# A transformer-and-recurrence step on one core: token-half norms, three tiles opened at once, a fourth weight slot

## The chip, the cores and the metric

The kernel runs on one core of a Trainium2 chip. A core has five engines that work side by side, each through its own instructions in order: TensorE (PE) multiplies matrices into PSUM, VectorE (DVE) and ScalarE (ACT) do elementwise work and read PSUM out, GpSimd (POOL) does elementwise work on SBUF, and SyncE (SP) issues most transfers. They meet only at semaphores. The metric is the device time of one execution in microseconds, the median of three runs.

## The reference

The reference is one inference step of a two-layer trunk. All tokens (16 meta, 512 prompt, 64 sample: 592 in all) go through one matrix product after another, and after each of the four sublayers stands a layer norm over the 1024 features, whose result is what the next product reads:

```
for layer in range(DEPTH):
    if layer % 2 == 0: m, ... = _mixer_ret_hgrn(x, ...)      # 32 tiles in, 8 tiles out
    else:              m, ... = _mixer_rglru(x, ...)         # 16 tiles in, 8 tiles out
    x = _layernorm(DEEPNORM_ALPHA * x + m, ...)              # norms 0 and 2
    f, nb = _conv_ffn(x, ...)                                # gelu(conv(x @ up_u)) * (x @ up_v), then @ down
    x = _layernorm(DEEPNORM_ALPHA * x + f, ...)              # norms 1 and 3

def _layernorm(x, g, b):
    mu = xf.mean(-1, keepdims=True)
    var = jnp.mean(jnp.square(xf - mu), -1, keepdims=True)
    return (xf - mu) * lax.rsqrt(var + LN_EPS) * g + b
```

## The kernel before

Features lie on the 128 partitions and tokens along the free axis, so x is eight rows of 592 tokens. Every weight matrix is cut into units: one unit gives 128 output features from eight (in a down-projection six or eight) blocks of 128 input features. Weights and activations are split into a high and a low part (`whi`, `wlo`, `xhi`, `xlo`, for the down-projections `hhi`, `hlo`), and `products` multiplies high by high, low by high and high by low: three matmuls of 296 columns for each block and each half of the tokens, so 48 matmuls for a unit of eight blocks. All units of the kernel stand in one sequence `u`.

The weights of a unit go through a chain: SP loads them into one of two `raw` buffers, ACT copies them to `whi` (`weights_hi`), DVE subtracts to get `wlo` (`weights_lo`), in one of three slots, and only then may PE begin the unit. Where `weights_hi(u + 2)` and `weights_lo(u + 2)` stand in the lists of ACT and DVE is written out by hand, unit by unit. The sums of a unit go to one of two accumulators in PSUM (two banks each, one for each token half); the semaphore `full` says that PE is done with it, `free` that ACT or DVE has read it.

A down-projection ends in a norm. Each of its last eight units adds to a row of `Y` (`add_tile`), DVE keeps the running sum Z0 and the sum of squares Z1, and ACT makes the squares. The last unit (`last_tile`) is done by token halves: first all blocks for tokens 0 to 295, then those for 296 to 591, with the matmuls that turn Z0 and Z1 into mean and mean square (`layer_norm_moments`, L675) for the first half after the sixth block of the second half. From there on the first half of the tokens goes through variance, Ln and Exp (for the reciprocal root), then row by row through DVE (subtract the mean L1308, scale L1311), ACT (bias L877, then `xhi` L879) and POOL (`xlo` L478). `first_tiles` opens the next two units together: at each block that arrives it does the products of both units for that half of the tokens, and in the second half the second unit runs three blocks behind.

After the norm ACT's list goes on with `weights_hi` of the third unit, then reads out the first unit (in a feed-forward network L912 to L918, in the recurrent mixer L984 to L989), then `weights_hi` of the fourth. DVE's list goes on with `weights_lo` of the third, then the convolution of the first unit, then `weights_lo` of the fourth. The feed-forward network has 22 u/v pairs of units in groups of 8, 8 and 6, each group followed by eight down units of as many blocks. Its `u` units are convolved, its `v` units multiplied by the gelu.

## Time and profile before

| | us |
|---|---|
| median of 3 runs | 1509.72 (1508.63 to 1510.45) |
| the profiled execution | 1509.73 |
| its span, first to last instruction | 1507.9 |
| PE busy in the span | 1439.3 |
| DVE busy | 849.3 |
| ACT busy | 622.7 |
| POOL busy | 61.0 |

The profiled execution lies 1.8 us over its span and agrees with the median. The busy share is an average over stages. To see what sets the time, look at the stretches around each norm and ask for each what PE waited for there; the stretches between the norms can be read in one row each.

### The profile page before, as it was taken

To read this page: it belongs to the slowest core of one execution; us is meant where nothing else is said; L and a number is where in the kernel's file an instruction comes from. 1 tells how busy PE (TensorE), PEld (TensorE's weight loads), DVE (VectorE), ACT (ScalarE), POOL (GpSimd) and SP (SyncE) were. 2 spreads that over 40 slices of the span, in tenths; PEclk is the share of its full clock that TensorE was granted. 3 is DMA by queue.
4 is the path that set the end of the run, shared out by engine and by line. 5 is a ranking of instruction groups with operands and counts; after the bars stand their busy time and mean duration, and the time that the engine had idled before them with its cause. 6 is when DMAs were issued, how large, how long until landed. Compare 5 with 4: busy or idle time off the path is not lost.

```text
span 1507.9 us, 24289 instructions
## 1 busy us (share of the span) xinstructions
PE 1439.3 (95%) x10240; PEld 1402.7 (93%) x10240; DVE 849.3 (56%) x1290; ACT 622.7 (41%) x1018; POOL 61.0 (4%) x80
## 2 busy tenths in 40 slices
PE   6999999999899999999999899998999999999993
PEld 6989898989899999999999799997999999999993
DVE  4566564755665554553355877868645344524556
ACT  4443544443464313341243676736543133313433
POOL 0010000000110000000000300002000000000000
PEclk9999999999999999999999999999999999999997
DMA  7132222323222222222222122121222222222222
GB/s 261 54 90 83 72 87 72 94 89 113 84 76 79 85 85 82 73 84 85 80 72 74 57 85 70 57 84 43 85 85 84 85 71 84 84 85 71 78 63 80
DMA packets 37085, 125.22 MB, mean 83 GB/s; under 512 B 4208, under 2 KB 6384, under 8 KB 36720
## 3 DMA queue, kind: packets, MB, share of 16 engines
q1 hardware_dynamic: 33264, 112.32, 23.3%
q0 software_dynamic: 2560, 8.91, 2.1%
q10 hardware_dynamic: 1152, 2.43, 0.5%
q8 instruction: 81, 1.33, 0.3%
q14 instruction: 28, 0.23, 0.0%
HBM read 115.95 MB, written 7.70 MB: 82 GB/s over the span
## 4 chain that ended last, share of the span: by engine, by line
PE 85%; DVE 6%; ACT 5%; DMA 1%; issue 1%; SPq 0%; POOL 0%; ACTq 0%; DVEq 0%
PE PS L486 26%; PE PS L487 26%; PE PS L488 26%; PE PS L713 1%; DMA C<-consts 1%; ACT Y L877 1%; PE PS L628 1%; ACT xhi L879 1%; PE PS L587 1%; DVE Y L1311 1%; DVE S L1209 1%; DVE wlo L1063 1%; PE PS L608 1%; DVE Y L1308 1%; PE PS L643 1%
## 5 line engine op out<-in xcount | busy, mean ns | idle before, releaser
L486 PE MATMUL PS<-xhi,whi 128*128 128x296 f32 x2176 | 668.8, 307 | 21.6 <-POOL xlo L478 6.9
L487 PE MATMUL PS<-xlo,whi 128*128 128x296 f32 x2176 | 656.1, 302 | 0.0
L488 PE MATMUL PS<-xhi,wlo 128*128 128x296 f32 x2176 | 653.3, 300 | 0.0
L486 PEld LDWEIGHTS PS<-xhi,whi 128*128 128x128 f32 x2176 | 413.9, 190 | 33.5 <-POOL xlo L478 14.6
L487 PEld LDWEIGHTS PS<-xlo,whi 128*128 128x128 f32 x2176 | 414.1, 190 | 1.2 <-issue 0.2
L488 PEld LDWEIGHTS PS<-xhi,wlo 128*128 128x128 f32 x2176 | 413.3, 190 | 0.0
L1063 DVE TENSOR_TENSOR wlo<-raw,whi 128x1024 fp32r<-128x1024 f32 (+1 forms) x198 | 238.2, 1204 | 111.8 <-ACT whi L744 108.4
L486 PE MATMUL PS<-hhi,whi 128*128 128x296 f32 x960 | 288.8, 301 | 4.2 <-ACT S L1015 3.0
L487 PE MATMUL PS<-hlo,whi 128*128 128x296 f32 x960 | 288.6, 301 | 0.0
L488 PE MATMUL PS<-hhi,wlo 128*128 128x296 f32 x960 | 287.5, 299 | 0.0
L744 ACT ACTIVATE whi<-raw 128x1024 fp32r<-128x1024 f32 (+1 forms) x198 | 206.5, 1043 | 175.2 <-PE PS L488 166.0
L486 PEld LDWEIGHTS PS<-hhi,whi 128*128 128x128 f32 x960 | 181.8, 189 | 5.4 <-issue 5.1
L487 PEld LDWEIGHTS PS<-hlo,whi 128*128 128x128 f32 x960 | 181.5, 189 | 0.4
L488 PEld LDWEIGHTS PS<-hhi,wlo 128*128 128x128 f32 x960 | 181.5, 189 | 0.0
L1345 DVE TENSOR_SCALAR S<-S,W 128x608 f32<-128x608 f32 x44 | 26.2, 596 | 149.9 <-ACT S L915 149.9
L925 ACT ACTIVATE hhi<-S 128x592 fp32r<-128x592 f32 x44 | 30.8, 700 | 145.4 <-DVE S L1359 145.4
L1348 DVE SCALAR_TENSOR_TENSOR S<-S,W 128x608 f32<-128x608 f32 x88 | 75.0, 852 | 3.1
L912 ACT ACTIVATE S<-W 128x16 f32<-128x16 f32 x44 | 9.6, 219 | 147.9 <-PE PS L488 147.9
L1273 DVE TENSOR_TENSOR Y<-PS,Y 128x592 f32<-128x592 f32 x30 | 23.3, 775 | 81.7 <-PE PS L488 81.7
L478 POOL TENSOR_TENSOR xlo<-Y,xhi 128x296 fp32r<-128x296 f32 x48 | 39.5, 823 | 666.0 <-ACT xhi L879 664.4
L853 ACT ACTIVATE S<-Y 128x592 f32<-128x592 f32 x28 | 19.6, 701 | 104.6 <-DVE Y L1271 58.1
L1271 DVE SCALAR_TENSOR_TENSOR Y<-Y,PS 128x592 f32<-128x592 f32 x30 | 23.1, 771 | 68.6 <-PE PS L488 68.4
(208 smaller groups left out, 1121.6 us busy)
## 6 DMA issues: line engine op xcount, KB each, us to landing
raw<-weights SPq DMA_DIRECT2D x182, 512.0 KB, 3.5
raw<-weights SPq DMA_DIRECT2D x16, 384.0 KB, 3.0
Y<-xP SPq DMA_DIRECT2D x8, 296.0 KB, 8.7
Y<-xT ACTq DMA_DIRECT2D x8, 296.0 KB, 4.1
yT<-Y SPq DMA_DIRECT2D x16, 148.0 KB, 1.8
C<-consts SPq DMA_DIRECT2D x1, 2146.5 KB, 15.3
S<-s_hgrn POOLq DMA_DIRECT2D x4, 512.0 KB, 4.6
S<-s_ret POOLq DMA_DIRECT2D x4, 512.0 KB, 4.8
```

The costliest lines, as they stand in the source:

```text
L478: pool.tensor_tensor(xlo[:, m, span(half)], Y[:, m, span(half)], xhi[:, m, span(half)].bitcast(F32), ALU.subtract).then_inc(x_lo, 1)
L486: pe.matmul(dst, wh, h, start=first, stop=False)
L487: pe.matmul(dst, wh, lo, start=False, stop=False)
L488: return pe.matmul(dst, wl, h, start=False, stop=last)
L744: act.activation(whi[:, u % SLOTS, 0:n], raw[:, u % RAWS, 0:n], ACT.Copy).then_inc(w_hi, 1)
L853: done(act.activation(s(T0 + m % 2), Y[:, m, :], ACT.Square), sq_ok)
L925: done(act.activation(hhi[:, j - first, :], s(4 + j % 2), ACT.Copy), h_hi)
L1063: tt(wlo[:, u % SLOTS, 0:n], raw[:, u % RAWS, 0:n], whi[:, u % SLOTS, 0:n].bitcast(F32), ALU.subtract).then_inc(w_lo, 1)
L1271: done(stt(y, y, ALPHA, a, ALU.mult, ALU.add), free[u % 2], u // 2 + 1)
L1273: done(tt(y, a, y, ALU.add), free[u % 2], u // 2 + 1)
L1345: done(ts(y, r[:, 0:n], par("ffn_conv_w", (layer * FW) * FT + j), par("ffn_conv_b", layer * FT + j), ALU.mult, ALU.add))
L1348: done(stt(y, r[:, q:q + n], par("ffn_conv_w", (layer * FW + q) * FT + j), y, ALU.mult, ALU.add), conv if q == FW - 1 else None)
```

## The change

1. The last two units of a down-projection are done by token halves (`last_tiles`): first half of both, then second half of both. The sums Z0 and Z1 for the first half are turned to moments after the fifth block of the second half of the last unit but one. For the second half of the tokens the last two rows are not added to Z0 and Z1: `moments_of_second_half` gives PE three rows to add up for each of mean and mean square, six matmuls in place of two. In norms 0 to 2 they stand in `first_tiles`, after its fourth step; in norm 3 right behind the last unit.
2. `first_tiles` opens three units in three accumulators. In the first half of the tokens they run 0, 3 and 6 blocks behind each other, in the second half side by side. The feed-forward networks go on with three accumulators, the mixers with two.
3. There are four weight slots in place of three, and the weights of the next three units are prepared earlier: `ahead` gives which at each of the last units. In `ffn` and in the mixer's loop `weights_hi(u + 2)` and `weights_lo(u + 2)` are left out for the first unit, so the fourth unit's come at the second.
4. DVE subtracts the mean for one or two rows at a time (`NORM_ROWS`), from a copy of the mean in SBUF that ACT makes; the reciprocal root stays in SBUF. ACT writes `xhi` for the rows of a group in one instruction. In norm 3 DVE only subtracts and multiplies, two rows at a time, and ACT applies gain and bias.
5. Groups of 6, 8 and 8 in place of 8, 8 and 6; in the recurrent mixer four gates and two decays come one unit later. `Sc` lies in rows of `S`.

```diff
-GROUPS = [8, 8, 6]
+GROUPS = [6, 8, 8]
...
-LAG = 3
+LAGS = [0, 3, 6]
+NORM_ROWS = [[(0, 1), (1, 2), (3, 2), (5, 2), (7, 1)], [(0, 2), (2, 2), (4, 2), (6, 2)]]
...
-GATES_AFTER = {2: 0, 3: 1, 5: 2, 6: 3, 9: 4, 10: 5, 12: 6, 13: 7}
+GATES_AFTER = {3: 0, 4: 1, 6: 2, 7: 3, 9: 4, 10: 5, 12: 6, 13: 7}
...
+def ahead(u, m):
+
+    return [u + 2] if m < KT - 3 else {KT - 3: [u + 2, u + 3], KT - 2: [u + 3], KT - 1: []}[m]
...
-        RAWS, SLOTS = 2, 3
+        RAWS, SLOTS = 2, 4
...
+            def last_tiles(u, ln):
+
+                n = unit_tiles(u)
                 for half in range(2):
+                    for i in range(2):
+                        for k in range(n):
+                            half_product(u + i, half, k, hhi, hlo, first_half)
+                            if half and i == 0 and k == n // 2:
+                                moments_of_first_half(ln)
+                if ln == 3:
+                    moments_of_second_half(ln)
...
+            def first_tiles(u, ln):
+
+                for half in range(2):
+                    lags = LAGS if half == 0 else [0, 0, 0]
+                    for step in range(KT + max(lags)):
+                        if step < KT:
+                            pe.wait_ge(x_lo, KT * (1 + 2 * ln + half) + step + 1)
+                        for i, lag in enumerate(lags):
+                            if 0 <= step - lag < KT:
+                                half_product(u + i, half, step - lag, xhi, xlo)
+                        if half == 0 and step == 3:
+                            moments_of_second_half(ln)
...
+            def moments_of_second_half(ln):
+
+                rows = [(s(Z0), Y[:, KT - 2, :], Y[:, KT - 1, :]), (s(Z1), s(T0), s(T1))]
+                pe.wait_ge(y_half, 4 * ln + 4)
+                pe.wait_ge(sq_ok, (KT + 2) * ln + KT + 2)
+                pe.wait_ge(mu_ok, 2 * ln + 1)
+                pe.wait_ge(var, 2 * ln + 1)
+                for i in range(2):
+                    for j, row in enumerate(rows[i]):
+                        mm = pe.matmul(PS[:, 6 + i, 0:HT], const("mean_d"), row[:, HT:T], start=j == 0, stop=j == 2)
+                mm.then_inc(ln_ps, 1)
...
+                square(KT - 2, 0)
+                square(KT - 1, 0)
+                mean(0)
                 root(0)
...
+                shifted(0, 0)
+                square(KT - 2, 1)
+                shifted(0, 1)
+                square(KT - 1, 1)
+                weights_hi(u + 3)
+                shifted(0, 2)
+                mean(1)
+                shifted(0, 3)
+                root(1)
+                shifted(0, 4)
+                for i in range(len(NORM_ROWS[1])):
+                    shifted(1, i)
...
-                    if i < N_FFN - 1:
+                    if kind == "d" and g == len(GROUPS) - 1:
+                        for v in ahead(u, j):
+                            weights_hi(v)
+                    elif i:
                         weights_hi(u + 2)
...
             for i, (kind, m) in enumerate(MIXER):
-                weights_hi(U_RNN + i + 2)
+                if i:
+                    weights_hi(U_RNN + i + 2)
...
                     if kind == "u":
-                        weights_lo(u + 2)
+                        if i:
+                            weights_lo(u + 2)
```

Three places show what moves. The first is ACT's list behind norm 0, where the first feed-forward unit is read out (the last rows of the norm are the pairs that end in `xhi`; `whi<-raw` is a unit's high weights). Before, the weights of the third unit and, behind the read-out, those of the fourth:

```order
L877 ACTIVATE Y<-Y,W 128x296
L879 ACTIVATE xhi<-Y 128x296
L744 ACTIVATE whi<-raw 128x1024
L912 ACTIVATE S<-W 128x8x2
L913 ACTIVATE S<-PS 128x8x8
L914 ACTIVATE S<-PS 128x296
L915 ACTIVATE S<-PS 128x232
L916 ACTIVATE KV<-PS 128x2
L918 ACTIVATE KV<-PS 128x16
L744 ACTIVATE whi<-raw 128x1024
L923 ACT_TABLE_LOAD
```

And in the changed kernel:

```order
L938 ACTIVATE Y<-Y,W 128x296 x2
L940 ACTIVATE xhi<-Y 128x2x296
L981 ACTIVATE S<-W 128x8x2
L982 ACTIVATE S<-PS 128x8x8
L983 ACTIVATE S<-PS 128x296
L984 ACTIVATE S<-PS 128x232
L985 ACTIVATE KV<-PS 128x2
L987 ACTIVATE KV<-PS 128x16
L799 ACTIVATE whi<-raw 128x1024
L992 ACT_TABLE_LOAD
```

The third unit's `whi` is gone from ahead of the read-out (it has moved into the norm), and the fourth unit's still stands behind it.

The second is DVE's list at the same place; `wlo<-raw,whi` is a unit's low weights, the rows on `S<-S,W` are the convolution of the first unit. Before:

```order
L1308 TENSOR_TENSOR Y<-Y,PS 128x296
L1311 SCALAR_TENSOR_TENSOR Y<-Y,W,PS 128x296
L1335 MEMSET S 128x2 x2
L1063 TENSOR_TENSOR wlo<-raw,whi 128x1024
L1345 TENSOR_SCALAR S<-S,W 128x608
```

And in the changed kernel:

```order
L1394 TENSOR_TENSOR Y<-Y,S 128x2x296
L1407 SCALAR_TENSOR_TENSOR Y<-Y,W,S 128x296 x2
L1435 MEMSET S 128x2 x2
L1446 TENSOR_SCALAR S<-S,W 128x608
L1449 SCALAR_TENSOR_TENSOR S<-S,W 128x608 x2
L1134 TENSOR_TENSOR wlo<-raw,whi 128x1024
```

The convolution now comes first, and the low weights behind it are the fourth unit's.

The third is ACT's list inside the norm. `S<-PS` is what reads the moments of the second half of the tokens. Before, it reads them behind the second row:

```order
L877 ACTIVATE Y<-Y,W 128x296
L879 ACTIVATE xhi<-Y 128x296
L865 ACTIVATE S<-PS 128x296
L877 ACTIVATE Y<-Y,W 128x296
L879 ACTIVATE xhi<-Y 128x296
```

And in the changed kernel, from the group of rows 1 and 2 on:

```order
L938 ACTIVATE Y<-Y,W 128x296 x2
L940 ACTIVATE xhi<-Y 128x2x296
L916 ACTIVATE S<-Y 128x296
L799 ACTIVATE whi<-raw 128x1024
L938 ACTIVATE Y<-Y,W 128x296 x2
L940 ACTIVATE xhi<-Y 128x2x296
L920 ACTIVATE S<-PS 128x296
L921 ACTIVATE S<-PS 128x296
L938 ACTIVATE Y<-Y,W 128x296 x2
```

The third unit's weights stand between rows 2 and 3, and the moments of the second half (L920 squares the mean, L921 copies it) ahead of rows 5 and 6. On PE those moments stand behind the products that wait for row 3:

```order
L523 MATMUL PS<-xhi,whi 128x296 [waits x_lo_ready]
L524 MATMUL PS<-xlo,whi 128x296
L525 MATMUL PS<-xhi,wlo 128x296
L523 MATMUL PS<-xhi,whi 128x296 [waits acc0_free,weights_lo]
L524 MATMUL PS<-xlo,whi 128x296
L525 MATMUL PS<-xhi,wlo 128x296
L734 MATMUL PS<-S,C 128x296 [waits ln_mean_in_sbuf,ln_var_ready,y_squared,last_tile_half_added]
L734 MATMUL PS<-Y,C 128x296 x2
L734 MATMUL PS<-S,C 128x296 x3
L523 MATMUL PS<-xhi,whi 128x296 [waits x_lo_ready]
```

Before, they stood at the end of the last unit, ahead of everything that `first_tiles` does.

## Rows read from the trace of the kernel before

**Rows 1.** The page's head: engine busy us (share) and instructions.

```profile
PE 1439.3 (95%) x10240; PEld 1402.7 (93%) x10240; DVE 849.3 (56%) x1290; ACT 622.7 (41%) x1018; POOL 61.0 (4%) x80
```

**Rows 2.** Table by stretches: start:end, length, busy us (instructions) by engine, PE clock, DMA.

```profile
386.90:432.31 45.41, 39.65 (x250) 35.73 (x249) 34.47 (x61) 30.93 (x57) 13.16 (x16) 0.96 0.17 52
834.96:877.76 42.80, 36.61 (x227) 32.61 (x226) 35.56 (x62) 29.64 (x60) 13.18 (x16) 0.96 0.19 57
1023.48:1068.46 44.98, 39.69 (x250) 36.06 (x249) 35.93 (x63) 30.82 (x57) 13.19 (x16) 0.96 0.15 50
1471.11:1507.90 36.79, 13.56 (x82) 11.68 (x80) 24.91 (x47) 15.01 (x27) 0.00 (x0) 0.70 0.23 82
432.31:834.96 402.65, 402.65 (x2955) 402.65 (x2953) 195.94 (x276) 134.56 (x240) 0.00 (x0) 1.00 0.26 81
```

**Rows 3.** Timeline of PE through norm 0: start, us, engine, line, [idle before <-releaser].

```profile
399.16 1.16 PE L675 MATMUL PS<-S,C 128*128 128x296 f32 x4
...
403.99 2.34 PE L675 MATMUL PS<-S,C 128*128 128x296 f32 x4 [2.85 <-DVE S L1254]
405.70 0.88 PE L486 MATMUL PS<-xhi,whi 128*128 128x296 f32 x1
...
425.68 0.37 PE L486 MATMUL PS<-xhi,whi 128*128 128x296 f32 x1 [0.30 <-ACT KV L918]
```

**Rows 4.** Timeline of ACT, DVE and POOL from the moments to the first x row.

```profile
400.35 0.42 ACT L865 ACTIVATE S<-PS 128x296 f32<-128x296 f32 x1 [1.34 <-PE PS L675]
401.36 0.54 ACT L870 ACTIVATE S<-S,C 128x296 f32<-128x296 f32 x1 [0.59 <-DVE S L1304]
403.52 0.54 ACT L877 ACTIVATE Y<-Y,W 128x296 f32<-128x296 f32 x1 [0.69 <-DVE Y L1311]
404.10 0.45 ACT L879 ACTIVATE xhi<-Y 128x296 fp32r<-128x296 f32 x1
...
402.91 0.52 DVE L1311 SCALAR_TENSOR_TENSOR Y<-Y,W,PS 128x296 f32<-128x296 f32 x1
...
404.70 0.81 POOL L478 TENSOR_TENSOR xlo<-Y,xhi 128x296 fp32r<-128x296 f32 x1 [51.07 <-ACT xhi L879]
```

**Rows 5.** Instructions over both halves of a row, DVE and ACT, before norm 0.

```profile
394.53 0.78 DVE L1278 TENSOR_TENSOR S<-S,Y 128x592 f32<-128x592 f32 x1
...
394.53 0.70 ACT L853 ACTIVATE S<-Y 128x592 f32<-128x592 f32 x1 [4.75 <-DVE Y L1271]
```

**Rows 6.** Timeline behind norm 0: read-out of the first unit, weights, convolution.

```profile
423.79 0.22 ACT L912 ACTIVATE S<-W 128x16 f32<-128x16 f32 x1 [0.73 <-PE PS L488]
...
425.57 1.06 ACT L744 ACTIVATE whi<-raw 128x1024 fp32r<-128x1024 f32 x1
...
425.15 0.60 DVE L1345 TENSOR_SCALAR S<-S,W 128x608 f32<-128x608 f32 x1 [0.76 <-ACT S L915]
425.79 1.74 DVE L1348 SCALAR_TENSOR_TENSOR S<-S,W 128x608 f32<-128x608 f32 x2
427.56 1.23 DVE L1063 TENSOR_TENSOR wlo<-raw,whi 128x1024 fp32r<-128x1024 f32 x1
```

**Rows 7.** Timeline of DVE behind norm 1: convolution of the mixer's first unit.

```profile
870.58 0.60 DVE L1437 TENSOR_SCALAR S<-S,W 128x616 f32<-128x616 f32 x1 [0.78 <-ACT S L987]
...
874.13 1.23 DVE L1063 TENSOR_TENSOR wlo<-raw,whi 128x1024 fp32r<-128x1024 f32 x1
```

**Rows 8.** Table by stretches around waits of PE (columns as in rows 2).

```profile
403.70:407.10 3.40, 3.12 (x8) 2.49 (x9) 2.42 (x6) 2.52 (x6) 1.62 (x2) 0.50 0.00 0
1485.70:1507.90 22.20, 2.34 (x4) 1.17 (x4) 15.97 (x33) 10.04 (x19) 0.00 (x0) 0.50 0.38 134
330.00:334.40 4.40, 1.66 (x13) 1.42 (x13) 1.27 (x3) 3.00 (x6) 0.00 (x0) 1.00 0.86 270
407.10:425.70 18.60, 15.69 (x94) 12.88 (x93) 14.95 (x31) 16.46 (x38) 11.53 (x14) 1.00 0.04 5
```

**Rows 9.** Timeline of ACT at the end: its last row.

```profile
1503.75 0.54 ACT L877 ACTIVATE Y<-Y,W 128x296 f32<-128x296 f32 x1 [0.51 <-DVE Y L1311]
```

More of the change, by code:

```diff
@@ new lines, in shifted @@
+                def shifted(half, i):
+                    first, n = NORM_ROWS[half][i]
+                    for m in range(first, first + n):
+                        act.wait_ge(ln_c, (2 * ln + half) * KT + m + 1)
+                        y, b = Y[:, m, span(half)], par(f"ln_{which}_b", layer * KT + m)
+                        if ln == 3:
+                            g = par(f"ln_{which}_g", layer * KT + m)
+                            done(act.activation(y, y, ACT.Identity, scale=g, bias=b), ln_x)
+                        else:
+                            done(act.activation(y, y, ACT.Identity, bias=b), ln_x)
```

305 lines of the change are left out of this document (163 added, 142 removed).

## The prediction, made before the changed kernel was run

> **What bounds the kernel now.** I read the page's head first: PE is busy 95% of the span, nothing else over 56% [rows 1]. So the time is PE's work plus the places where PE has none, and the change can gain only in those. The table by stretches says where they are [rows 2]. The stretch between two norms (432.31 to 834.96, and one of the same length in the second layer) is busy to the last 0.01 us: 2955 matmuls in 402.65 us, 0.1363 us each. The four stretches around the norms are not. For each I start where the last unit but one of the down-projection starts (call this point S) and stop where the fourth unit after the norm starts. By the number of matmuls such a stretch should take five units, 32.71 us at 48 x 0.1363 (29.44 in norm 1, whose two last units have six blocks), and it took 45.41, 42.80 and 44.98: 12.70, 13.36 and 12.27 us over. In the last stretch there are 9.81 us of units, and with 36.79 us it is 26.98 over. Those 65.3 us are what the change works on.
>
> Then I looked at what PE waits for in one of them. In norm 0 PE waits 2.85 us for the sum of squares of the second half, and works on x from 405.70 on at the pace at which rows arrive; at the third unit it waits 0.30 us more [rows 3]. The row's path is ACT, DVE, ACT, POOL [rows 4].
>
> **Parts that cost or gain nothing.** The third accumulator and the fourth slot inside the feed-forward networks remove no wait, since the stretch is full [rows 2]. Groups of 6, 8, 8 hold the same blocks as 8, 8, 6; what moves is 3.27 us of units into stretch 2 and into the last, which the count "over the units" takes care of. The first down units now take 6 x 6 x 0.1363 = 4.91 us; DVE's three or four operations there, 0.8 to 1.2 us each [rows 5, 6], fit. The heads' order is as before.
>
> **Norm 0, step by step.** All times are from S.
>
> Both first halves are full at 48 x 0.1363 = 6.54. DVE and ACT then need add, sum, square, add again; by their durations at one half (about 0.47 each) the sums are there at 8.2. PE comes to the first moments 15 matmuls after 6.54, at 8.59, and doesn't wait. This is the part that works: 33 of the 96 matmuls are still to come and cover the chain; PE's last one ends at 14.3 (96 x 0.1363 and 1.2 for the moments). In the old order the path from moments to the first matmul on x took 405.70 - 399.16 = 6.54 us [rows 3]; the new one loses one DVE subtract ahead of it and takes 6.2. So x row 0 is used at 14.8: PE waits 0.5 us where it waited 2.85 and then for 1.7 us of moments.
>
> But then PE lives on arrivals. For each row ACT spends 0.54 on the bias and 0.45 on `xhi` (0.70 for two rows at once) [rows 4, 5], POOL 0.81 [rows 4]. Into the same ACT list the change puts two squares (0.45 each) and the third unit's high weights (1.06 [rows 6]) ahead of row 3. Walked one after the other: rows 1, 2 and 3 reach PE at 17.1, 17.9 and 20.3. PE has 0.41 us of products for each of rows 0 to 2 (only the first unit is open), so it waits 1.7, 0.3 and 1.9 us.
>
> Now the second moments. They are six matmuls where there were two. Two took 399.16 to 400.35, the first products behind them starting 0.77 us after [rows 3, 4], so I take 0.25 for each half of one and 12 x 0.25 = 3.0 us. They stand on PE behind row 3, from 21.2 to 24.2. ACT reads them ahead of the bias of rows 5 and 6, so all of ACT's list waits for PE: mean squared and mean (0.42 each), two biases, one `xhi`, POOL; row 5 is there at 28.3. PE has used up row 4 by 25.1 and waits 3.2 us. In the old order the moments needed nothing from `first_tiles`.
>
> From 28.3 on PE has enough to do: 17 products of three matmuls left in the first half, 24 in the second, 41 x 0.409 and about a tenth of a us for each of eleven waits: 46.2.
>
> There the second halves of all three units end together. The fourth unit needs its weights. ACT's list has the read-out of the first unit, then `weights_hi`; DVE's has its convolution, then `weights_lo` (both as the order shows). The first unit is full 0.82 us before 46.2; read-out to L915 takes 423.79 to 425.12, convolution 0.60 and 1.74, weights 1.23 [rows 6]: 46.2 - 0.8 + 0.2 + 1.4 + 2.4 + 1.2 + 0.2 = 50.8. PE waits 4.6 us. Before, this wait was 0.30, as the third unit's weights stood ahead of the read-out and the third unit's 6.54 us covered the rest.
>
> So the fourth unit starts at 50.8, 18.1 over its units, against 12.7: **5.4 us lost**. Walked by the same durations the old order comes out 0.3 us short of its trace.
>
> **Norm 1** has the same walk, but the mixer's convolution is longer (870.58 to 874.13, 3.5 us [rows 7]): the last wait is 5.7, 19.2 over against 13.4: **5.8 lost**. In **norm 2** DVE restores three rows of x (0.78 each [rows 5]) and makes two `wlo` while the unit ahead of S runs, and is about 1.3 us late: 18.7 over against 12.3: **6.4 lost**. Together 17.6.
>
> **The clock.** After a wait of 2.85 us PE ran at half its clock (1.2 GHz) for 3.4 us [rows 3, 8]; each of the three stretches shows this as a mean of 0.96 [rows 2]. After a wait of 2.74 at 330 to 334 it did not, nor in the stretch full of waits under 0.9 (407.10 to 425.70) [rows 8]. In the new order each norm has two waits longer than the 2.85 that half clock followed (3.2 and 4.6) and PE is dense behind both, so each stretch of half clock costs up to half of 3.4, 1.7 us. I take 1.25 for each of two, less the 0.3 of the old order: 2.2 a norm, **6.6 in all**; the bounds are 0 and 1.7 x 3 x 3 = 15, with a third one over the loose stretch from 14 to 21, where PE is busy a third of the time.
>
> [...]
>
> **Norm 3.** The chain of the first half is the same up to 12.0. Behind it stands no PE work but 3.0 us of moments, which wait for the last squares until 16.0 (DVE's add and ACT's square behind 14.3). DVE's work on two rows is 0.78 + 0.78 where it was four of about 0.5; ACT (0.54 a row) keeps up. The second moments end at 19.0, variance and root 2.2 us later; then four groups of 1.6 on DVE, and ACT's last two: 29.2. The old list ended at 1504.29 [rows 9], 33.2 from S, with 3.27 less of units. From the end of ACT to the end of the span stay 3.6 us. So 16.1 over against 23.4: **7.3 gained**, less 0 to 3 for moments at half clock (they took 2.34 for four there [rows 3]); I take 1.0, **6.3**.
>
> **The sum** against the profiled time: 1509.7 + 17.6 + 6.6 - 6.3 = 1527.6, and the median of the runs is the same 1509.7. I say 1527.5.
>
> **Rivals.**
> (a) Faster: the head start does what it is for, so that waits end with row 3. This needs the moments read without holding ACT's list and the fourth unit's weights ready. Then PE is dense from 20.3: 45 products, 3.0 of moments and 1.3 of small waits end at 43.0, and the fourth unit starts at 43.5, 10.8 over: 1.9, 2.6 and 1.5 gained, with the end 12 us, 1497.5. For it: PE has the work. Against it: both orders are written out, and engines don't overtake in their lists. It decides if the two waits of 3.2 and 4.6 us shrink by more than 6 us together in each norm, a third of the 17.9 that the sum is over. 4%.
> (b) Only the fourth unit's weights come in time: 14 us less wait and half of the clock's cost, 1510 to 1513, about as before. Against: the same list. 6%.
> (c) More is lost than I count: half clock three times a norm, 9 us more, 1536. For it the loose stretch; against it rows 8's 407.10 to 425.70, busy 84% though. 17%.
> (d) The mixer falls behind: DVE's second convolution stands behind the fourth unit's weights while PE goes on at once, and by the order ACT loads its tables 16 times there for 14. A list that gets behind by one convolution, 3.5 us [rows 7], can make PE wait once for a gate or for a free accumulator: 0 to 3.5 us more. I count nothing, as the fourth unit's own 6.5 us and a gate's products cover it. Otherwise 1531. 13%.
> The forecast itself, 1521 to 1533: 60%.
>
> **How the numbers follow.** The range is 1517 to 1537: below, no clock cost (1521) less an error of 1 us a norm; above, most of (c). What this kernel's measurement can tell from no change is about 0.2%, 3 us. Faster by more: (a), 4%, and a miss in the same direction, 2%: 6%. Within: (b), 5%. Slower: 89%.
>
> **What would show it.** The trace of the changed kernel should have, in each of norms 0 to 2, a wait of about 0.5 us at the first product on x; one near 3.2 us at the products for row 5, with ACT idle until the six-matmul moments end; and 4 to 6 us before the fourth unit, with `wlo` as releaser. Stretches of half clock behind those two. From S to the fourth unit it should take about 53, 54 and 53.5 us. The dense stretches should stay at 0.1363 a matmul. From the last matmul of the last unit to the end: about 18.5 us, where it was some 25. If the wait before the fourth unit is missing, I have misread the lists; if the wait for row 5 is missing, the moments or what stands behind them are cheaper than I think.

## The result, and the profile after

The changed kernel is slower: a median of 1542.39 us in four runs against 1509.43 for the kernel before beside it, a ratio of 1.0213 (95%: 1.0194 to 1.0231). Its four runs lie in two pairs, 1538.27 and 1538.78, 1546.01 and 1546.43. The profiled one is 1538.78, and everything below explains that one. Run again as e0 it gave 1537.78 (1536.35 to 1538.77), without the upper pair. So the forecast of 1527.5 is 10 to 15 us short, and the time lies outside the range that ended at 1537.

The head of the profile after, engine busy us (share) and instructions, answers to [rows 1]:

```profile
PE 1453.8 (95%) x10272; PEld 1418.3 (92%) x10272; DVE 854.8 (56%) x1251; ACT 628.7 (41%) x1011; POOL 66.1 (4%) x80
```

PE is busy 14.5 us longer. The 32 more records are the added matmuls of the second moments, four in each norm with two records each, 8.0 us at the 0.25 of the forecast. The other 6.5 us are work that was there before and now takes longer.

The table by stretches of the kernel after, with columns as in [rows 2]: the stretch from S to the fourth unit in norms 0, 1 and 2, the end, and then the stretch between norms 0 and 1, which in the kernel before was full and at full clock:

```profile
388.03:441.35 53.32, 41.84 (x258) 38.45 (x256) 34.57 (x48) 28.33 (x50) 14.89 (x16) 0.88 0.11 34
842.93:897.01 54.08, 40.65 (x259) 37.61 (x257) 35.66 (x50) 29.56 (x58) 14.90 (x16) 0.93 0.10 32
1045.41:1099.50 54.09, 42.09 (x259) 38.96 (x257) 35.56 (x50) 28.31 (x50) 14.90 (x16) 0.89 0.11 33
1501.36:1537.00 35.64, 19.14 (x114) 16.95 (x112) 20.49 (x32) 17.65 (x30) 0.00 (x0) 0.78 0.24 84
441.35:842.93 401.58, 401.58 (x2928) 401.58 (x2929) 199.19 (x281) 137.28 (x243) 0.00 (x0) 0.99 0.27 83
```

With them the account of the span (1507.9 to 1537.0, 29.1 us more) closes:

| | before | after | difference |
|---|---|---|---|
| up to S of norm 0 | 386.90 | 388.03 | +1.1 |
| S to fourth unit, norms 0 to 2 | 45.41, 46.07, 44.98 | 53.32, 54.08, 54.09 | +25.0 |
| between the norms (three stretches) | 399.38, 145.72, 399.38 | 401.58, 148.40, 401.86 | +7.4 |
| S of norm 3 to the end | 40.06 | 35.64 | -4.4 |

Where units moved with the groups, the 3.27 us that they take are put where they are now: norm 1 before is 42.80 + 3.27, the end 36.79 + 3.27, and the long stretches 402.65 - 3.27.

The third line is new. Most of it is the clock. The stretch behind the fourth unit splits like this (same view, after):

```profile
439.10:445.92 6.82, 4.57 (x18) 4.57 (x19) 5.47 (x9) 5.23 (x10) 0.00 (x0) 0.50 0.26 77
448.00:842.90 394.90, 394.90 (x2897) 394.90 (x2896) 193.93 (x273) 132.89 (x234) 0.00 (x0) 1.00 0.27 82
```

From 439.1 to 445.9 PE has half its clock, 1.2 GHz, and for the last 4.57 us of it PE is dense, which costs 2.3. Then 394.90 us go by at 0.1363 a matmul as before. In the trace of the kernel before, each of norms 0 to 2 has one stretch of half clock of 3.4 us. Now norm 0 has 10.2 us (from 405.0) and 6.8 us (from 439.2), norm 1 has 6.8 and 3.4, norm 2 has 6.8, 3.4 and 6.8.

The waits, on the other hand, are the forecast's. Timeline of PE through norm 0 after (as [rows 3]): the first products on x rows 0, 1 and 3, the six matmuls of the second moments, the first product on row 5, and the first of the fourth unit:

```profile
402.67 0.40 PE L523 MATMUL PS<-xhi,whi 128*128 128x296 f32 x1 [0.42 <-POOL xlo L515]
405.25 0.61 PE L523 MATMUL PS<-xhi,whi 128*128 128x296 f32 x1 [1.91 <-POOL xlo L515]
409.18 0.61 PE L523 MATMUL PS<-xhi,whi 128*128 128x296 f32 x1 [1.83 <-POOL xlo L515]
410.83 1.19 PE L734 MATMUL PS<-S,C 128*128 128x296 f32 x2
...
413.78 2.40 PE L734 MATMUL PS<-S,C 128*128 128x296 f32 x6
419.92 0.41 PE L523 MATMUL PS<-xhi,whi 128*128 128x296 f32 x1 [2.93 <-POOL xlo L515]
441.35 0.61 PE L523 MATMUL PS<-xhi,whi 128*128 128x296 f32 x1 [4.40 <-DVE wlo L1134]
```

Two things are to be seen. The waits are 0.42, 1.91, 1.83, 2.93 and 4.40. And the matmul at 405.25 takes 0.61 where a full-clock one takes 0.40: from row 1 on PE is at half clock, and the six moments, which start at 410.83, are done only 5.4 us later, at 416.2, when ACT can read them.

ACT's side of the wait for row 5, and ACT's and DVE's sides of the wait for the fourth unit, in the timeline of norm 0 after:

```profile
416.22 0.42 ACT L920 ACTIVATE S<-PS 128x296 f32<-128x296 f32 x1 [8.33 <-PE PS L734]
...
437.20 0.37 ACT L984 ACTIVATE S<-PS 128x232 f32<-128x232 f32 x1
...
438.02 1.06 ACT L799 ACTIVATE whi<-raw 128x1024 fp32r<-128x1024 f32 x1
...
437.67 0.60 DVE L1446 TENSOR_SCALAR S<-S,W 128x608 f32<-128x608 f32 x1 [6.84 <-ACT S L984]
438.30 1.74 DVE L1449 SCALAR_TENSOR_TENSOR S<-S,W 128x608 f32<-128x608 f32 x2
440.07 1.22 DVE L1134 TENSOR_TENSOR wlo<-raw,whi 128x1024 fp32r<-128x1024 f32 x1
```

ACT is idle for 8.33 us although rows 5 to 7 of the first half wait for it: its next instruction reads the mean of the second half, which PE has not yet made. Later DVE is idle for 6.84 us and then does the convolution ahead of the `wlo` that PE is waiting for. This is the whole list effect. The second moments are also where the slow clock hurts a second time, since ACT waits for them.

The last piece stands in the groups of instructions: line, engine, operation, count | busy us, mean ns of one. After, the POOL low part and the DVE scale by the reciprocal root:

```profile
L515 POOL TENSOR_TENSOR xlo<-Y,xhi 128x296 fp32r<-128x296 f32 x48 | 44.7, 949 | 690.8 <-ACT xhi L940 690.8
L1407 DVE SCALAR_TENSOR_TENSOR Y<-Y,W,S 128x296 f32<-128x296 f32 x48 | 40.3, 840 | 4.7 <-ACT S L927 3.2
```

and the same two groups of the kernel before:

```profile
L478 POOL TENSOR_TENSOR xlo<-Y,xhi 128x296 fp32r<-128x296 f32 x48 | 39.5, 823 | 666.0 <-ACT xhi L879 664.4
L1311 DVE SCALAR_TENSOR_TENSOR Y<-Y,W,PS 128x296 f32<-128x296 f32 x64 | 33.5, 523 | 2.3
```

The same operations on the same shapes have become dearer on both engines, 823 to 949 ns and 523 to 840. The one difference is that the root is now read from SBUF (`Y<-Y,W,S` for `Y<-Y,W,PS`).

### The profile page after: what moved, and what is told of

It is laid out like the page before. It is cut to its first block, busy times and chain, and to the rows that moved or that the text cites. A ratio compares the mean times of both kernels' runs of the same rounds, so it can differ in the third digit from the quotient of the medians.

```text
span 1537.0 us, 24403 instructions
## 1 busy us (share of the span) xinstructions
PE 1453.8 (95%) x10272; PEld 1418.3 (92%) x10272; DVE 854.8 (56%) x1251; ACT 628.7 (41%) x1011; POOL 66.1 (4%) x80
## 4 chain that ended last, share of the span: by engine, by line
PE 82%; DVE 9%; ACT 5%; issue 1%; DMA 1%; SPq 0%; POOL 0%; ACTq 0%; DVEq 0%
PE PS L523 25%; PE PS L524 25%; PE PS L525 25%; DVE wlo L1134 1%; PE PS L734 1%; DMA C<-consts 1%; PE PS L675 1%; DVE Y L1407 1%; PE PS L634 1%; DVE S L1280 1%; PE PS L655 1%; PE PS L690 1%; DVE S L1540 1%; ACT whi L799 1%; DVE S L1577 1%
## 5 line engine op out<-in xcount | busy, mean ns | idle before, releaser
L523 PE MATMUL PS<-xhi,whi 128*128 128x296 f32 x2176 | 670.2, 308 | 50.9 <-POOL xlo L515 22.3
L1134 DVE TENSOR_TENSOR wlo<-raw,whi 128x1024 fp32r<-128x1024 f32 (+1 forms) x198 | 237.9, 1204 | 93.6 <-ACT whi L799 89.6
L515 POOL TENSOR_TENSOR xlo<-Y,xhi 128x296 fp32r<-128x296 f32 x48 | 44.7, 949 | 690.8 <-ACT xhi L940 690.8
L1457 DVE TENSOR_TENSOR S<-PS,S 128x296 f32<-128x296 f32 x44 | 20.5, 466 | 68.2 <-PE PS L525 68.2
```

The lines of the kernel that those rows point to most:

```text
L515: pool.tensor_tensor(xlo[:, m, span(half)], Y[:, m, span(half)], xhi[:, m, span(half)].bitcast(F32), ALU.subtract).then_inc(x_lo, 1)
L523: pe.matmul(dst, wh, h, start=first, stop=False)
L1134: tt(wlo[:, u % SLOTS, 0:n], raw[:, u % RAWS, 0:n], whi[:, u % SLOTS, 0:n].bitcast(F32), ALU.subtract).then_inc(w_lo, 1)
L1457: done(tt(ht[:, 0:HT], a[:, 0, 0:HT], y[:, 0:HT], ALU.mult))
```

## The experiments

Eleven kernels were run. The questions were: how much does each of the two list waits cost, how much the clock, is anything else in the change good or bad, and can it be mended? Unless it is said otherwise, a diff is against the changed kernel. Each ratio is to the kernel before, run beside it.

### e0: the changed kernel again

> The changed kernel once more, in five rounds. Its four runs lay in two groups, 1538.3 and 1538.8, and 1546.0 and 1546.4, with mean clocks of 0.977 and 0.972. Theory (the clock): the two groups come again, about 8 us apart, since how much of the norms PE does at half clock depends on where its waits fall. Rival (the chip of those runs): one group only. From the second last unit to the fourth after the norm the profile should have 53.3, 54.1 and 54.1 us again if it falls in the lower group.

Measured: 1537.78 (1536.35 to 1538.77), ratio 1.0177 (1.0162 to 1.0192). The profiled execution of the first result belongs to this group. The two groups that were expected did not come again, so the expectation's rival (one group only) held. All differences below are taken to 1537.8.

### e1: the fourth unit's weights ahead of the read-out

```diff
@@ ACT, ffn
-                    elif i:
+                    elif i == 0:
+                        weights_hi(u + 3)
+                    elif i > 1:
                         weights_hi(u + 2)
@@ DVE, ffn
-                        if i:
-                            weights_lo(u + 2)
+                        weights_lo(u + (2 if i else 3))
...
-                        weights_lo(u + 2)
+                        if i > 1:
+                            weights_lo(u + 2)
```

and in the mixer's loops likewise.

> The changed kernel with the fourth unit's high and low weights ahead of the read-out and the convolution of the first unit, in the two networks and the mixer. Theory (the lists): the waits before the fourth unit (4.4, 5.6 and 4.4 us on wlo) shrink to 1.2 to 1.3 each, which are the read-out of the first unit, whose accumulator the fourth takes; 10.5 us less. With the shorter waits the half clock behind them, which cost about 2.4 us each outside the stretch, goes too: 7 us more, so 1521. Rival (the lists behind are late): ACT and DVE have the read-outs of three units to do, and the fifth or sixth unit waits instead, so that most comes back: 1532 or more.

Measured: 1524.25 (1523.61 to 1526.01), ratio 1.009 (1.0075 to 1.0105), so 13.5 us less. Waits of PE in e1, by what they wait for: us, count, mean; and the stretch of norm 0:

```profile
PE PS L523 <- POOL xlo L515: 21.9, 13, 2.9
...
PE PS L523 <- ACT KV L989: 2.2, 2, 1.1
```

```profile
387.69:437.71 50.02, 41.85 (x258) 38.45 (x257) 33.21 (x45) 26.13 (x48) 14.89 (x16) 0.90 0.15 48
```

In the kernel after the same view has this, with the wait for `wlo` second:

```profile
PE PS L523 <- POOL xlo L515: 22.3, 14, 2.9
...
PE PS L523 <- DVE wlo L1134: 14.4, 3, 5.6
```

Three waits of 4.40 to 5.6 us, 14.4 together, have turned into three of 1.1 for the read-out of an accumulator (`KV`), and the waits for rows are almost untouched (21.9 for 22.3). The stretches took 50.02, 49.59 and 50.51. The half clock behind the fourth unit is gone. The wait has two successors, though. Besides the 1.1 us for the accumulator, the two feed-forward networks now wait for the fifth unit's weights, since those come one convolution later:

```profile
PE PS L523 <- DVE wlo L1136: 3.3, 2, 1.7
```

So the three stretches are 11.4 us shorter and the long ones behind them keep 401.41 (399.38 before): the 2 us of half clock that went were taken by this wait. That is why it is 1524 and not the 1521 expected. The mechanism of the forecast's last wait is confirmed.

### e2: ACT reads the second moments two groups of rows later

```diff
@@ ACT
-                mean(1)
                 shifted(0, 3)
-                root(1)
                 shifted(0, 4)
+                mean(1)
+                root(1)
```

with DVE's `variance(1)` behind its fifth group to match.

> The changed kernel with ACT reading the second moments (mean, then variance and root) behind rows 5, 6 and 7 in place of ahead of rows 5 and 6, and DVE's variance moved the same way. Theory (ACT's list waits for PE): the wait for row 5 (2.9 us in each of three norms) goes and nothing takes its place, since PE has 41 block products ahead: 8.8 us less, 1530, and up to 4 less if a stretch of half clock goes with it. Rival: the root of the second half comes later and PE waits for its first rows instead, 1 to 3 us each: 1535 to 1538.

Measured: 1527.07 (1522.35 to 1527.82), ratio 1.01 (1.0083 to 1.0117), 10.7 us less. Waits of PE in e2:

```profile
PE PS L523 <- DVE wlo L1134: 14.4, 3, 5.6
PE PS L523 <- POOL xlo L515: 13.7, 11, 2.3
```

The waits for rows fall from 22.3 to 13.7, by 8.6 us (three of 2.92 are 8.8), and those for `wlo` don't move. The stretches took 50.16, 50.81 and 49.62. The wait at row 5 was indeed ACT standing at the moments. The stretches give 10.9 us. The end gives 2.1 more, 33.53 for 35.64 (0.3 of it by the edit, which reaches norm 3 too, the rest by the clock; see e5), and the mixer behind norm 1 takes 2.6 back, with a stretch of half clock of 6.8 us from 998.3 where the kernel after has 3.4.

### e5: the waits kept, the clock held

The kernel after with matmuls of constants put into PE's waits, whose result nothing uses: four ahead of rows 1 and 3, eight ahead of row 5, twelve ahead of the fourth unit in each of norms 0 to 2.

```diff
+            def filler(n, out):
+                for _ in range(n):
+                    pe.matmul(out, const("mean_d"), const("cos", 0, 200), start=True, stop=True)
...
+                        if half == 0 and step == 1:
+                            pe.wait_ge(free[ACC[u + 2]], NTH[u + 2])
+                        if half == 0:
+                            filler({1: 4, 3: 4, 5: 8}.get(step, 0), acc[ACC[u + 2]][:, 0, 0:200])
...
+                filler(12, PS[:, 6, 0:200])
```

> The changed kernel with added matmuls on a constant, whose result nobody reads, put in where PE waits: 4 ahead of rows 1 and 3, 8 ahead of row 5, 12 ahead of the fourth unit, in norms 0 to 2 (84 fp32 matmuls of 200 columns, 0.33 us each). They do no work of the computation. Theory (the clock is the part that I had too small): PE stays at full clock in the norms, the second moments take 3 us in place of 6 and the fourth unit starts at 0.1363 us a matmul: 2.5 us inside each stretch and 2.4 behind it, 14 to 15 us less, 1524. Rival (the waits alone): the clock stays or the fillers themselves cost what they save: 1538 or more.

Measured: 1522.58 (1520.38 to 1523.05), ratio 1.0072 (1.0055 to 1.0089), **15.2 us less with added work**. The stretches of the three norms in e5 (the last number but two is the clock; a constant matmul has two records, so 28 of them are some 56 more):

```profile
387.24:437.62 50.38, 47.92 (x315) 45.02 (x313) 34.53 (x48) 28.23 (x50) 14.88 (x16) 1.00 0.11 36
837.13:888.67 51.54, 47.90 (x314) 45.02 (x313) 35.64 (x50) 29.46 (x58) 14.90 (x16) 1.00 0.11 35
1036.94:1087.83 50.89, 48.19 (x314) 45.05 (x312) 35.64 (x50) 28.24 (x50) 14.91 (x16) 1.00 0.11 36
```

The clock is 1.00 in all three, where it was 0.88, 0.93 and 0.89. DVE's, ACT's and POOL's columns are those of the kernel after: nothing was moved but PE's own time. The second moments in e5:

```profile
409.31 0.66 PE L743 MATMUL PS<-S,C 128*128 128x296 f32 x2
...
410.81 1.66 PE L743 MATMUL PS<-S,C 128*128 128x296 f32 x6
412.08 0.52 PE L523 MATMUL PS<-xhi,whi 128*128 128x296 f32 x1
```

ACT's read of them begins at 412.50, 3.2 us after their start, about as the prediction had it (3.0), against 5.4 in the kernel after. PE still stood or ran fillers for 4.55, 5.77 and 4.55 us ahead of the fourth unit, so the waits on the other engines are unchanged. Between the two profiled executions (1538.78 and 1523.05) the 15.7 us are: 8.6 in the three stretches (2.9, 2.5, 3.2), 4.4 in the two long stretches, which are back at 399.51 and 399.52, 1.8 in the end, 0.1 in the mixer and 0.8 ahead of S of norm 0, where there are no fillers and which stays unexplained. The end has no fillers either, but there it is the clock. Timeline of PE at the end of e5, the second moments of norm 3:

```profile
1503.54 0.74 PE L743 MATMUL PS<-S,C 128*128 128x296 f32 x2 [1.97 <-issue]
...
1505.11 1.66 PE L743 MATMUL PS<-S,C 128*128 128x296 f32 x6
```

3.2 us, where the kernel after needs 4.9 for them (its rows stand below). Whether these moments fall into a stretch of half clock seems not to depend on the work around them: in after, e1, e2, e4, e5 and e9 they start 16.2 us behind S, after the same work. The end took 35.6 us in after, e1 and e6, 33.9 in e5, 34.4 in e9 and 33.5 to 33.6 in e2, e3, e4 and e10, whose edit has ACT read the moments of norm 3 later too and accounts for 0.3. This is the disputed cost by itself: **half clock costs about 15 us here**, 13.0 of which the fillers themselves took out (8.6 and 4.4). The prediction had put 7.6 in its sum (6.6 and 1.0 for norm 3), with 15 and 3 as bounds.

### e3: e1 and e2 together

The edits of both, and no other.

> Both moves of order together: the fourth unit's weights ahead of the read-out, and ACT's and DVE's reading of the second moments behind rows 5 to 7. Alone they took 13.5 and 10.7 us off 1537.8. Theory (two separate waits): they add up, 1513 to 1514, still above the kernel before, because the loose stretch at rows 0 to 3 and the longer moments stay. Rival (each frees the other's cover): less than the sum, 1518 or more.

Measured: 1512.49 (1511.78 to 1518.05), ratio 1.0015 (1.0006 to 1.0024). From e0 that is 25.3 us less, where 13.5 and 10.7 add up to 24.2. The stretches took 46.40, 46.08 and 47.23. So the two waits account between them, with the clock that each of them brings, for nearly all that the change lost; but 2.0 of the 25.3 are the end, where most of it is where the clock happened to fall. The profiled execution is 2.3 us over that of the kernel before: 3.3 more in the three stretches, 4.1 in the long ones (401.41 each, the waits for the fifth unit), 1.5 in the mixer and ahead of the first norm, and 6.5 less at the end.

### e4: e3, and the units staggered in the second half too

```diff
@@ against e3
-                    lags = LAGS if half == 0 else [0, 0, 0]
+                    lags = LAGS
```

> As the one with both moves, and the second half of the tokens with units 3 and 6 blocks behind each other as the first half has. Theory: the first unit is full 2.5 us before the third's last block, so its read-out (1.2 us exposed in each norm) is covered, and rows of the second half have fewer products waiting on them: 3 to 4 us less than with both moves alone, about 1510, near the kernel before. Rival: with rows of the second half arriving every 1.4 us (POOL and DVE block each other) PE runs out of products and waits there: no gain or a loss, 1513 to 1516.

Measured: 1509.53 (1508.58 to 1511.18), ratio 0.9993 (0.9984 to 1.0002), the same as before. The first unit now ends earlier than the others, and its read-out is done when PE wants the accumulator: the wait before the fourth unit is 0. The long stretches are back at 399.38 and 399.39. For that small waits for rows come back in the second half (0.32, 0.78 and 0.51 us in norm 0), since PE again runs at their pace, and the three stretches take 48.16, 47.93 and 47.28, 6.9 us more than before and 3.7 more than in e3. What e4 gains on e3 comes from the long stretches (4.1) and the mixer (145.05 for 146.62). Against the kernel before, the end, 33.59 for 40.06, pays for the stretches.

### e6: only two units opened

```diff
-LAGS = [0, 3, 6]
+LAGS = [0, 3]
...
-                    lags = LAGS if half == 0 else [0, 0, 0]
+                    lags = LAGS if half == 0 else [0, 0]
```

The third unit is done like any other. All else is as in the changed kernel.

> The changed kernel with two units opened together in place of three (0 and 3 blocks behind in the first half, side by side in the second), all else as changed, the third unit behind them. Theory: the third unit's 6.5 us cover the fourth unit's weights, so the 14.4 us of waits before the fourth unit go; but in the first half PE has fewer products behind row 5, and the third unit's start waits for the read-out of nothing (a third accumulator is free): 10 to 13 us less than changed, 1525 to 1528. Rival (three opened is what the gain rests on): PE waits for rows in both halves as before, and the time stays above 1532.

Measured: 1526.89 (1526.19 to 1528.52), ratio 1.0102 (1.0087 to 1.0117). Waits of PE in e6 have no entry for `wlo` L1134, and for rows

```profile
PE PS L523 <- POOL xlo L515: 26.6, 23, 2.9
```

Without the third unit the waits for rows rise by 4 us (22.3 to 26.6) and the wait of 4.4 to 5.6 before the fourth unit goes, since the third unit's own 6.5 us cover it. Taken as it was written, opening three units cost 11 us: it gave PE 4 us of work while rows were missing, and took away the cover of the next step. The clock behind the fourth unit is part of the 11: the long stretches take 399.40 each here for 401.58 and 401.86.

### e7: the groups alone, in the kernel before

```diff
-GROUPS = [8, 8, 6]
+GROUPS = [6, 8, 8]
```

> The kernel before with groups of 6, 8, 8 alone. Theory: two units of 8 blocks ahead of norms 1 and 3 cover DVE's running sums, so the wait of 0.79 and 0.85 us at the first moments goes, and 12 more matmuls cover the chain of the first half: 1.6 to 2.5 us less, 1508.5 to 1509.5 beside 1511.0. Rival: nothing that the rounds can tell (within 0.5 us).

Measured: 1508.27 (1506.36 to 1509.65), ratio 0.998 (0.9972 to 0.9989), 2.4 us less. In its waits of PE

```profile
PE PS L675 <- DVE S L1254: 11.9, 4, 3.3
```

where the kernel before has six such waits of 13.6 us together.

Two blocks more in the last unit cover two of the waits for the last sums. The prediction had counted the groups at nothing in the changed kernel, where last units are done by halves and such waits are gone. That isn't contradicted; the part is a small gain only on its own.

### e8: the root in SBUF, in the kernel before

```diff
-                    done(act.activation(PS[:, 6 + half, 0:HT], v, ACT.Exp, scale=-0.5), ln_r)
+                    done(act.activation(v, v, ACT.Exp, scale=-0.5), ln_r)
...
-                    done(stt(y, y, par(f"ln_{which}_g", layer * KT + m), rstd_of[half], ALU.mult, ALU.mult), ln_c)
+                    done(stt(y, y, par(f"ln_{which}_g", layer * KT + m), s(T1)[:, span(half)], ALU.mult, ALU.mult), ln_c)
```

> The kernel before with the reciprocal root written to its row in SBUF in place of PSUM, so that DVE's scale reads two operands from SBUF. Theory (DVE and POOL hold each other up when both read SBUF): DVE's scale grows from 0.52 us to about 1.0 where POOL runs beside it and POOL's low part from 0.82 to 0.9 and more, rows arrive every 1.4 us in place of 1.05, and each of norms 0 to 2 gets 1 to 4 us longer: 1514 to 1520 beside 1510.7. Rival: the slower rows of the changed kernel come from its two-row groups, and here the durations and the time stay.

Measured: 1514.99 (1513.08 to 1516.64), ratio 1.0026 (1.0016 to 1.0037), 4.5 us more. The two groups of instructions in e8:

```profile
L478 POOL TENSOR_TENSOR xlo<-Y,xhi 128x296 fp32r<-128x296 f32 x48 | 46.3, 990 | 663.8 <-ACT xhi L879 663.8
L1311 DVE SCALAR_TENSOR_TENSOR Y<-Y,W,S 128x296 f32<-128x296 f32 x64 | 36.1, 564 | 2.3
```

One operand moved from PSUM to SBUF, the same count of instructions and the same values, and POOL's operation goes from 823 to 990 ns; PE's waits for `xlo` go from 6.9 to 9.9 us. I had expected DVE's operation to bear it, at about 1 us. It goes only from 523 to 564: in this order of work POOL bears it. The total and the mechanism held, the engine didn't. Of the 4.5 us 3.0 are waits; norms 0 and 1 also have one stretch of half clock more, of 3.4 us each (from 421.5 and from 861.8), so part of the rest is the clock.

### e9: e4 with fillers ahead of rows 1 and 3

Four constant matmuls, whose result nothing uses, ahead of each of the two rows in each of norms 0 to 2, by the `filler` of e5.

> The one with both moves and lags in both halves, with 4 added fp32 matmuls on a constant ahead of row 1 and of row 3 in norms 0 to 2 (24 matmuls of 200 columns that compute nothing that is used). Theory (half clock over the moments is what keeps that kernel from gaining): the moments take 3 us in place of 6 and the products behind them full clock: 3 us less in each norm, 1500 to 1502. Rival: the rows then are what PE waits for, and it gives back more than half: 1505 or more.

Measured: 1505.59 (1503.09 to 1512.9), ratio 0.9975 (0.9963 to 0.9986). **Faster than both kernels**, if only by 0.25% against the kernel before, and short of the 1500 to 1502 expected; it lies where the rival put it (1505 or more). The stretch of norm 0 in e9 (norms 1 and 2: 45.25 and 45.73, clock 1.00 too):

```profile
387.67:432.94 45.27, 41.73 (x274) 38.54 (x273) 33.64 (x47) 26.65 (x49) 15.36 (x16) 1.00 0.16 52
```

The clock stays at 1.00. The stretches are 7.1 us shorter than e4's, where 9 were expected, and only 4 came out between the profiled executions (2.7 by the two ratios): the mixer took 1.6 back (146.62 for 145.05, with a stretch of half clock of 3.4 us at 985.0 that e4 doesn't have), the end 0.8 and the head 0.6. With 45.3 a stretch is only level with the kernel before (45.41, 46.07, 44.98), in spite of the head start. What e9 has over the kernel before is the end of the program.

### e10: e9 with the third unit's weights two rows later

```diff
@@ ACT, against e9 (DVE likewise)
-                weights_hi(u + 3)
                 shifted(0, 2)
+                weights_hi(u + 3)
```

> As the one before it, with the third unit's weights behind rows 3 and 4 in ACT's list and behind rows 5 and 6 in DVE's, in place of ahead of them. Theory: row 3 arrives 1.0 us earlier, PE's wait there shrinks by as much, and the third unit needs its weights only at its first block: 1 us less in each norm at most, 0 to 3 us less than with the fillers alone. Rival: the weights then hold up the rows behind, and nothing changes (within 1 us).

Measured: 1506.27 (1505.48 to 1507.98), ratio 0.9969 (0.9958 to 0.9981), the same as e9, with stretches of 45.75, 45.71 and 46.21. So the rival held. The 1.06 us of weights ahead of row 3 are not what holds row 3 up in e9: ACT writes the `xhi` of rows 3 and 4 19.1 us behind S in both. Row 3 still reaches PE 0.4 us earlier (20.8 for 21.1 behind S), since POOL's two operations there take 1.82 for 2.17, and the time doesn't follow. Rows 0 to 3 still come at DVE's and POOL's pace, and what of the 45.3 goes to the six-matmul moments, to these rows and to DVE against POOL was not taken apart further.

## Why the prediction was wrong

**The heads, the groups, the slots.** Counted at nothing; +1.1 us up to S of norm 0. Right enough.

**The head start and the waits up to row 3.** Forecast 0.5, 1.7, 0.3 and 1.9; measured 0.42, 1.91, next to nothing and 1.83 in norm 0. Norms 1 and 2 begin the same way (0.39, 1.91, 0.33) and their wait for row 3 is 2.26 and 1.83. Right.

**The wait for row 5.** Forecast 3.2 by ACT's list standing at the moments; measured 2.93, 2.92, 2.92, with the releaser and ACT's idle time as named. e2 takes it out. Right. It didn't come out longer although the moments took 5.4 us in place of 3.0, because both what PE still has to do (row 4) and what ACT has to do for row 5 start only when the moments are done: slow moments put both off alike, and their price is PE's own time.

**The wait before the fourth unit.** Forecast 4.6, and 5.7 at the mixer; measured 4.40, 5.62, 4.41, released by `wlo`. e1 takes it out. Right.

**The sum of the ordering.** Forecast 17.6. The three stretches grew by 25.0, and e5 shows 8.6 of these to be clock, which leaves 16.4. Right within 1.2. (The kernel before had half clock in these stretches too, 0.3 each by my estimate. Net of that, as the forecast counted, it is 17.3 for 17.6, and 13.7 for 6.6 in the next term.)

**The clock.** This is the term that failed. I took 1.25 us for each of two stretches of half clock in a norm, less 0.3 for the one there was: 6.6 together. It cost 8.6 in the stretches, 2.2 and 2.5 in the long stretches behind norms 0 and 2, and 1.3 behind norm 1 (from 897.01 to 900.00 PE did 12 matmuls, at a clock of 0.51, where 22 fit at 0.1363), 14.6 together. Three steps were wrong. I had the half clock behind the two long waits, and behind the one for row 5 it came only in norm 2 (1077.4 to 1080.8); in norm 0 the product at 419.92, right behind that wait, takes 0.41 us, and the clock is 1.00 from there to the wait for the fourth unit. I took from [rows 8] that a stretch of half clock lasts 3.4 us, and it lasted 6.8 and 10.2 where the loose work went on or, before the fourth unit, where it began in the middle of the wait (439.2). And I took the row of small waits, 407.10 to 425.70 with PE busy 84%, as the nearest to the new loose stretch, though I had PE busy only a third of the time in the latter, and it was busy half of it (4.43 of the 8.57 us from 402.26 to 410.83, most of them at half clock). There the half clock begins at 405.0, in the wait for row 1, at a wait of 1.91 us, shorter than the 2.74 that left the clock alone in [rows 8]. The length of one wait is not what decides. The kernel after shows this row, from the wait for row 1 to the middle of the moments:

```profile
404.96:415.20 10.24, 8.13 (x21) 6.17 (x22) 5.35 (x6) 2.45 (x4) 3.39 (x4) 0.50 0.18 52
```

The waits in this stretch are 1.91 and 1.83 us, with 0.7 and 2.1 us of products ahead of them. The case that the Trainium skill describes ("TensorE: Matmul & The Clock Gate", section "HAM oscillation — how this bites in real kernels") is another: there groups of matmuls of about 2 us stand between waits of 3 to 5 us, and each wait throttles PE again. The waits of this stretch are shorter than those, and the trace shows half clock all the same.

With 14.6 for 6.6 the sum is 1535.6. My rival (c), half clock three times a norm with the third in the loose stretch, 1536 and 17%, was the case that came nearest.

**Norm 3.** Forecast 7.3 less 1.0, 6.3; measured 4.4. Timeline of the end after, PE's second moments and a pair of ACT's biases:

```profile
1517.56 1.13 PE L734 MATMUL PS<-S,C 128*128 128x296 f32 x2 [1.98 <-issue]
...
1520.46 2.02 PE L734 MATMUL PS<-S,C 128*128 128x296 f32 x6
...
1532.07 1.30 ACT L936 ACTIVATE Y<-Y,W 128x296 f32<-128x296 f32 x2 [0.42 <-DVEq L1403]
```

The moments wait 1.98 us for the last squares, as the walk had it, and then run at half clock for 3.4 of their 4.9 us: 1.8 us by the comparison with e5, where the term stood at 1.0. At full clock the gain is 6.2 (40.06 less 33.85 of e5) for the 7.3 forecast. ACT takes 0.65 a row for its bias (1.30 for two) where I had put 0.54, and the pairs of DVE 1.73 where I had put 1.6.

**What was missed.** That DVE and POOL get in each other's way. The prediction took 0.52 for the scale and 0.81 for `xlo` from [rows 4], but the mean and the root had moved into SBUF. Timelines of DVE and then of POOL after, in norm 0, around two subtractions of two rows (L1394):

```profile
403.58 0.78 DVE L1394 TENSOR_TENSOR Y<-Y,S 128x592 f32<-128x592 f32 x1
404.39 1.12 DVE L1407 SCALAR_TENSOR_TENSOR Y<-Y,W,S 128x296 f32<-128x296 f32 x1
405.55 0.97 DVE L1407 SCALAR_TENSOR_TENSOR Y<-Y,W,S 128x296 f32<-128x296 f32 x1
...
404.38 0.81 POOL L515 TENSOR_TENSOR xlo<-Y,xhi 128x296 fp32r<-128x296 f32 x1 [1.77 <-ACT xhi L940]
405.15 1.04 POOL L515 TENSOR_TENSOR xlo<-Y,xhi 128x296 fp32r<-128x296 f32 x1
...
426.14 1.54 DVE L1407 SCALAR_TENSOR_TENSOR Y<-Y,W,S 128x296 f32<-128x296 f32 x2
427.72 1.28 DVE L1394 TENSOR_TENSOR Y<-Y,S 128x592 f32<-128x592 f32 x1
...
426.25 2.12 POOL L515 TENSOR_TENSOR xlo<-Y,xhi 128x296 fp32r<-128x296 f32 x2 [0.77 <-ACT xhi L940]
```

At 403.58 POOL has nothing to do and the subtraction takes 0.78, as in [rows 5]. At 427.72 POOL is at work and the same subtraction takes 1.28; the two scales from 404.39 on, with POOL beside them, take 1.12 and 0.97 for 0.52. Look at where they end: at 405.51 and 406.52, 0.32 us behind the end of POOL's operation each time (405.19 and 406.19), and POOL's second ends 0.68 behind the first scale. It moved the waits little (1.91 for 1.7), because ACT's list and PE's moments set the pace behind it, so it isn't the cause of the miss; in e8, where the root alone moved, 3.0 us of waits came of it, in a kernel 4.5 us slower.

**The other rivals.** (a) and (b) would have needed the lists to be otherwise: e1 is (b) made true, and with it the kernel is still 13 us slower than the kernel before, not level with it: 6.6 us of new waits (for the accumulator and for the fifth unit) take the place of the old, and the half clock in the loose stretch stays. (d), the mixer falling behind, came true in part: PE waits once for a gate there, 1.4 us that the kernel before doesn't have, inside the 0 to 3.5 that the rival gave. Waits of PE after:

```profile
PE PS L768 <- DVE Y L1547: 1.4, 1, 1.4
```

I had counted nothing for it.

So the sum closes: 1527.6, and 8.0 for the clock, 1.4 for the gate, 1.9 for norm 3, 1.1 for the head, less 1.2 for the ordering, is 1538.8. What remains open is the upper pair of runs at 1546: it was not profiled and did not come again. Their mean clock in the records was 0.972 where it was 0.977 in the lower pair, so more half clock is probably part of it, but that is not shown, and why is not known.

## What to carry to other kernels

A wait of PE has two prices, the wait and the clock in and behind it. In a stretch like this one, groups of 0.7 to 2.1 us between waits of nearly 2 us, count on half clock, price the work in it at half speed, and add the dense work behind a long wait (3.0 to 5.2 us of it at half clock behind the waits for the fourth unit here). Waits under 0.9 us in work that is otherwise dense did not bring it ([rows 8]). When the matmul engine is given more work for a loose stretch, look at what that work used to cover: here the third unit's 6.5 us had hidden the next weights, and opening it early turned the cover into a wait of 4.4. In a list written out by hand, an instruction that reads something PE makes in the middle of its own waiting belongs behind everything that PE is waiting for.

## What the runs showed of the hardware

Work that computes nothing can pay. In e5 the fillers, 28 matmuls in each norm, kept the granted clock at 1.00 in the norms with the same waits on other engines; the kernel was 15.2 us faster, 13.0 of it in the norms and the long stretches behind them. In e9, 8 in each norm gave about 3 to 4 us.

Where a stretch of half clock falls can depend on what happened long before it: the second moments of norm 3, the same instructions in the same order, took 4.9 us in the kernel after and 3.2 in e5, which differs only in norms 0 to 2. Nearly 2 us of the end hang on that, and neither kernel's text shows it.

From the start of the same six fp32 matmuls to ACT's read of them took 3.2 us at full clock (e5) and 5.4 where nearly all of it was half (after).

Where DVE reads two operands from SBUF while POOL does too, one of the two waits for the other. One operand moved from PSUM to SBUF (e8) took POOL's operation from 823 to 990 ns and DVE's from 523 to 564; in the changed kernel, where both mean and root had moved, it was 823 to 949 and 523 to 840. In the kernel after, each of the 24 scales that begin while POOL is at work ends 0.32 or 0.33 us behind the end of POOL's operation, whether it took 0.95 or 1.13 us, where one with POOL idle takes 0.53. In the kernel before, with the root in PSUM, it takes 0.52 beside POOL and without it. Who bears the wait depends on the order of work. The Trainium skill has the mechanism ("SBUF — State Buffer", section "Who interferes with whom": a DVE instruction with two SBUF inputs contends with a GpSimd instruction that reads SBUF, and whichever issues first holds the port pair for its whole length). The traces agree: the delay appears only where the second operand is in SBUF, and the fixed 0.32 us behind POOL's end is what waiting for the whole of its operation looks like.
